# x loaded by halves of its columns, the small first loads on ScalarE's queue, the first weight tile in two halves

## The reference

```python
h = rms_norm(x, a_norm[layer])
att = diff_attention(h, a_w_qkv[layer], ...)     # begins with h @ w_qkv, then norms and rotations of q and k
x = x + att @ a_w_o[layer]
```

## Time and profile before

| | |
|---|---|
| time, median of 3 runs | 1870.19 us (1869.36 to 1870.36) |
| span of the profiled execution, first to last instruction | 1867.2 us |
| median of the timed runs less that span | 3.0 us |
| TensorE busy | 1783.1 us (95%) |
| VectorE busy | 1111.0 us (60%) |
| ScalarE busy | 926.1 us (50%) |
| GpSimd busy | 281.4 us (15%) |
| mean granted TensorE clock | 0.983 |

### The profile page before, as it was taken

How to read it: one execution, slowest core, us unless ns; L and a number is a source line. 1 busy time by engine, 2 the same in 40 slices (tenths; PEclk the granted TensorE clock), 3 DMA queues, 4 the chain that set the end, 5 groups by cost and what they waited for, 6 DMA issues and landing times.

```text
span 1867.2 us, 23188 instructions
## 1 busy us (share of the span) xinstructions
PE 1783.1 (95%) x9282; PEld 1497.2 (80%) x9282; DVE 1111.0 (60%) x1473; ACT 926.1 (50%) x1202; POOL 281.4 (15%) x209
## 2 busy tenths in 40 slices
PE   7778999979999999999999999999999999999997
PEld 5557999868887779998888887888888888888886
DVE  6676655666666656555476474655565667546554
ACT  5354444545655555444564545544455454554442
POOL 2620000066678610000200000000012000000000
PEclk9889999989999999999999999999999999999999
DMA  7223555443433425555754543555665544535561
GB/s 256 91 90 105 192 195 185 159 148 124 135 118 131 136 68 196 188 180 177 241 188 160 177 161 113 177 184 186 196 207 181 174 169 158 180 110 195 188 194 68
DMA packets 158746, 302.64 MB, mean 162 GB/s; under 512 B 5467, under 2 KB 52960, under 8 KB 158640
## 3 DMA queue, kind: packets, MB, share of 16 engines
q1 hardware_dynamic: 157520, 297.16, 47.9%
q0 software_dynamic: 1120, 4.00, 0.8%
HBM read 300.09 MB, written 1.05 MB: 161 GB/s over the span
## 4 chain that ended last, share of the span: by engine, by line
PE 81%; DVE 10%; ACT 4%; POOL 2%; issue 2%; DMA 0%; SPq 0%; DVEq 0%; ACTq 0%; POOLq 0%
PE ps L389 21%; PE ps L391 21%; PE ps L390 21%; PE ps L359 4%; PE ps L581 3%; PE ps L583 3%; PE ps L582 3%; DVE wlo L1217 3%; ACT whi L806 2%; ACT work L886 1%; DVE mx L1298 1%; PE ps L455 1%; PE ps L770 1%; POOL work L1800 1%; DVE st L1283 1%
## 5 line engine op out<-in xcount | busy, mean ns | idle before, releaser
L1217 DVE TENSOR_TENSOR wlo<-raw,whi 128x2048 fp32r<-128x2048 f32 x280 | 657.2, 2352 | 498.5 <-ACT whi L806 498.2
L389 PE MATMUL ps<-whi,hT_hi 128*128 128x512 f32 (+1 forms) x2000 | 794.3, 397 | 8.4 <-DVE wlo L1217 3.8
L391 PE MATMUL ps<-whi,hT_lo 128*128 128x512 f32 (+1 forms) x2000 | 779.4, 390 | 0.0
L390 PE MATMUL ps<-wlo,hT_hi 128*128 128x512 f32 (+1 forms) x2000 | 778.4, 389 | 0.0
L806 ACT ACTIVATE whi<-raw 128x2048 fp32r<-128x2048 f32 x280 | 535.7, 1914 | 387.8 <-PE ps L391 332.0
L389 PEld LDWEIGHTS ps<-whi,hT_hi 128*128 128x128 f32 x2000 | 378.3, 189 | 90.4 <-issue 11.1
L391 PEld LDWEIGHTS ps<-whi,hT_lo 128*128 128x128 f32 x2000 | 377.2, 189 | 79.3
L390 PEld LDWEIGHTS ps<-wlo,hT_hi 128*128 128x128 f32 x2000 | 378.5, 189 | 72.6
L581 PE MATMUL ps<-hT_hi,whi 128*128 128x256 f32 x512 | 145.1, 283 | 0.2
L583 PE MATMUL ps<-hT_hi,wlo 128*128 128x256 f32 x512 | 144.9, 283 | 0.0
L582 PE MATMUL ps<-hT_lo,whi 128*128 128x256 f32 x512 | 144.9, 283 | 0.0
(11 more groups left out here) (162 smaller groups left out, 1224.6 us busy)
## 6 DMA issues: line engine op xcount, KB each, us to landing
raw<-in_w_in SPq DMA_DIRECT2D x46, 1024.0 KB, 5.1
raw<-in_w SPq DMA_DIRECT2D x88, 512.0 KB, 4.5
raw<-in_m_w_up SPq DMA_DIRECT2D x32, 1024.0 KB, 5.2
raw<-in_m_w_down SPq DMA_DIRECT2D x32, 1024.0 KB, 4.9
raw<-in_kv_w SPq DMA_DIRECT2D x24, 1024.0 KB, 5.2
raw<-in_w SPq DMA_DIRECT2D x22, 1024.0 KB, 4.9
raw<-in_a_w_qkv SPq DMA_DIRECT2D x12, 1024.0 KB, 5.8
raw<-in_b_w_q SPq DMA_DIRECT2D x12, 1024.0 KB, 5.1
```

What stands on the lines that cost most here:

```text
L389: pe.matmul(acc, xh, wh, start=start and k == 0, stop=False)
L390: pe.matmul(acc, xh, wl, start=False, stop=False)
L391: ins = pe.matmul(acc, xl, wh, start=False, stop=stop and k == kc - 1)
L1217: vec.tensor_tensor(wlo[:, m % SPLIT, :], raw[:, m % RAW, :], whi[:, m % SPLIT, :], ALU.subtract).then_inc(*mark("lo_ready", ("lo", m)))
```

## The change

The three small first loads move from SyncE to the head of ScalarE's list. x is loaded in four pieces, 512 columns of 128 rows each, and its second half is issued behind tile 0; the turns of a half wait for that half alone. Tile 0 is loaded in two halves (K blocks 0 and 1, then 2 and 3), and ScalarE and VectorE split it in two halves. TensorE begins tile 0 when the first half is split, and waits for the second at K block 2.

```diff
         def x_ready(v, t, n):
-            return ("xload",) if v == 0 else ("x", v, t, n)
+            return ("xload", n) if v == 0 else ("x", v, t, n)
...
         def _(sp):
-            for dst_ap, src, key in ((grows[0:N1, 0, :], a["rows"][0:N1], None), (grows[0:N2, 1, :], a["rows"][N1:N1 + N2], None),
-                                     (ident[:], a_c["c_ident"], ("constants",))):
-                sp.dma_start(dst_ap, src).then_inc(*mark("constants_loaded", key, 16))
-            for t in range(T):
-                last = sp.dma_start(x[:, t, :], a["x"][0, t * P:(t + 1) * P, :])
-                last.then_inc(*mark("x_loaded", ("xload",) if t == T - 1 else None, 16))
             for m, (kc, cols, srcs) in enumerate(tiles):
...
+                if m < 2:
+                    for t in range(T):
+                        last = sp.dma_start(x[:, t, m * 512:(m + 1) * 512], a["x"][0, t * P:(t + 1) * P, m * 512:(m + 1) * 512])
+                        last.then_inc(*mark(f"x_loaded{m}", ("xload", m) if t == T - 1 else None, 16))
+                if m == 0:
+                    src = srcs[0][0]
+                    sp.dma_start(view[:, 0:2], src[:, 0:2]).then_inc(*mark("first_half_landed", ("landed half",), 16))
+                    sp.dma_start(view[:, 2:4], src[:, 2:4]).then_inc(*mark(f"tile_landed{slot}", ("landed", 0), 16))
+                    continue
...
-                pe.wait_ge(*at("lo", m))
+                pe.wait_ge(*(at("lo", m) if m else at("lo half")))
...
+                            if m == 0 and t == 0 and k == 2:
+                                pe.wait_ge(*at("lo", 0))
...
+            def split_first():
+                for half, landed, key in ((slice(0, 1024), ("landed half",), ("hi half",)), (slice(1024, 2048), ("landed", 0), ("hi", 0))):
+                    act.wait_ge(*at(*landed))
+                    sc.activation(whi[:, 0, half], raw[:, 0, half], CP).then_inc(*mark("hi_ready", key))
...
+            for dst_ap, src, key in ((grows[0:N1, 0, :], a["rows"][0:N1], None), (grows[0:N2, 1, :], a["rows"][N1:N1 + N2], None),
+                                     (ident[:], a_c["c_ident"], ("constants",))):
+                act.dma_start(dst_ap, src).then_inc(*mark("constants_loaded", key, 16))
...
             x_half(0, 0)
-            split(0)
+            split_first()
             x_half(0, 1)
...
+            def split_first():
+                for half, landed, hi, lo in ((slice(0, 1024), ("landed half",), ("hi half",), ("lo half",)),
+                                             (slice(1024, 2048), ("landed", 0), ("hi", 0), ("lo", 0))):
+                    dve.wait_ge(*at(*landed))
+                    dve.wait_ge(*at(*hi))
+                    vec.tensor_tensor(wlo[:, 0, half], raw[:, 0, half], whi[:, 0, half], ALU.subtract).then_inc(
+                        *mark("lo_ready", lo))
...
             x_half(0, 0)
-            split(0)
+            split_first()
             x_half(0, 1)
```

## The result

The changed kernel takes 1872.26 us (median of 20 runs, 1871.49 to 1873.93) against 1869.71 us before (20 runs beside it, 1868.78 to 1870.66): ratio 1.0015, 95% interval 1.0008 to 1.0021. It is slower by 2.55 us. The spans of the two profiled executions go the same way: 1870.3 against 1867.2.

A forecast was written before the change was run, and what follows sets the result against it. Mostly TensorE work after a start-up chain through x's load, ScalarE and VectorE. Turns 1.55 earlier plus split 0.5 minus later loads 0.2 gives 1.85 us, so 1870.19 becomes 1868.3 us, range 1865.3 to 1872.2.

The forecast's parts named there:

- ident issued at 1.80, landed 6.26 as before: Small loads on ScalarE's queue: ident keeps SyncE's issue and landing times, so the turns of x start at 7.5.
- The rule against the change: First loads: queues share 16 DMA engines, so spreading saves only issue time; priced at gain 1.5 us, time 1868.7.
- The bound above for ident: Latest case for the first turns: ident issued after ScalarE's table load, 1.28 us later, turns at 8.8.
- X: Start of TensorE's turns of x's first half, 9.05 before; forecast 7.5, bounds 6.3 to 8.8.
- the rival by which nothing moves: First loads land as before, set by the chip's start; only the split's 0.5 us or less is left; chance 0.07.
- ScalarE's table load: Rival at ScalarE's start: table load precedes the small loads, ident issued at 3.1, gain only 0.75 us, 1869.4; chance 0.08.
- x by halves: Load of x: first half lands at 5.6, latest 6.6, so ident sets the turns at 7.5, 1.55 us earlier.
- Both come earlier by between 0 and 1.47: x half 1 and tile 1, landing 11.55 and 14.15 at the same bytes before, were to come that many us earlier.
- Tile 0 in halves: ScalarE and VectorE split of tile 0: saves about 0.5 us on the chain at lo of tile 1.
- From there to lo of tile 2 is VectorE work of fixed length: VectorE between lo of tile 1 and tile 2 (19.83 to 29.30): gain passes through whole, tile 2 at 27.4.
- TensorE's clock: Rival at tiles 2 and 3: 2.2 us wait drops the clock; a 3.4 us fall costs 1.7; chance 0.12 including later stretches.
- The rival that the clock helps: Half-clock stretches between 60 and 660 us end sooner, each 3.4 us giving another 1.7 us, 1866.6; chance 0.18.

The follow-up runs named there:

- e4: Changed kernel, but SyncE waits for ident before its first load, so ScalarE's small loads have the DMA engines to themselves; profiled span 1869.8 us.
- e2: Kernel before, with only the three small loads moved to ScalarE's queue; ratio to before 1.0022.
- e3: Changed kernel, with the first gain-row load taking 128 rows instead of 113; ratio to before 0.9996.
- e5: Changed kernel with small loads back on SyncE and gain rows as 128 rows, halves kept; ratio to before 0.9993.
- e6: Kernel before, with only the gain rows loaded as 128 rows instead of 113; ratio to before 0.9993.
- e3b: Same kernel as e3, run again for its trace alone; profiled span 1864.9 us, restart at 65.58 in e3 and 66.38 here.
- e10: e3 with VectorE's two waits for the landing of tile 0's halves left out; ratio to before 0.9998.
- e1: Changed kernel with the three small loads back at the head of SyncE's queue, halves kept; ratio to before 0.9995.
- e1b: Same kernel as e1, run again for its trace alone; profiled span 1866.5 us, restart at 66.99.
- e7: Kernel before, with only tile 0 loaded and split in halves; profiled span 1867.6 us.
- e12: Kernel before plus 128 gain rows and tile 0 in halves without VectorE's landing waits, TensorE waiting for whole tile 0; 1866.72 us, ratio 0.9986.
- e9: e1 with TensorE waiting for both halves of tile 0 before its first matmul; profiled span 1868.4 us.
- e8: e5 with all four quarters of x issued ahead of tile 0; ratio to before 0.9993.
- e13: Kernel before, with two tiny clears added on VectorE ahead of lo of tile 0; profiled span 1867.9 us.
- e11: Kernel before, with two waits for long-arrived semaphores added on VectorE ahead of lo of tile 0; profiled span 1867.6 us.

## Why the prediction was wrong

**The step that failed: "ScalarE issues the same three from 0.74 ... so I take SyncE's times: ident issued at 1.80, landed 6.26 as before".** The issue time was right (1.86); the landing was 10.80. The load shares the DMA engines with SyncE's bulk, and its last packets drip behind x and tile 0. e4 (no bulk: 5.95), e2 (the queue alone: 12.83) and e3 (128 rows instead of 113: 6.56) show both halves of it: the sharing, and the gain rows that come one behind the other. In SyncE's own queue they had gone ahead of the bulk. With the rows as 128 only the sharing is left: ident was used 1.8 to 2.0 us after its issue from SyncE's queue (e5, e6) and 4.7 to 5.3 from ScalarE's (e3, e3b, e10).

**The rule against the change was named and priced too low.** I put its price at "as late as the first x block of before (6.6)". Two things were missed: that a small load beside a large one loses time at each of its packets (25 ns alone, 95 beside the bulk), and that the packets were not evenly spread, which the trace of before already showed as 75 small packets in line while x was moving. The bound above for ident (X at 8.8, for another mechanism) was not the upper end; X came at 11.98. Nor was 3.2 us from issue to landing the lower one: in e5 and e6 ident was in use 1.8 and 2.0 us after its issue. That also rules out the rival by which nothing moves because the start sets the landings.

**ScalarE's table load** went behind the three issues, so this rival falls, by the timeline above.

**x by halves.** X at 7.5 came about once ident was in time, at 7.27 and 7.65 in e1 and e1b, but partly by luck. The first half was put at 5.6, at the latest at 6.6, and that was too early: in the changed kernel its second load landed at 1.2 + 6.1 = 7.3, which the late ident hid, and in e1 the turns waited for x and not for ident. "At worst each is about 0.4 late" for the second half was wrong as well: in e1 it was used at 11.72 where X + 3.1 = 10.4 wanted it, 1.3 us late, in e5 2.6. "Both come earlier by between 0 and 1.47" failed in the changed kernel: x's last quarter landed at 12.1 (8.6 us after an issue near 3.5), tile 1 at 4.09 + 10.8 = 14.9, both later than the 11.55 and 14.15 at the same number of bytes before. It is the 113-row load again and not the order: e3 differs from the changed kernel in that load alone, and there the two landed at 9.8 and 12.5, 1.7 ahead of before (10.2 and 13.0 in e10). None of this reached the time of the changed kernel, where nothing waited for them: of the signs of being wrong, "x half 1 landing after 11.5" came true without being the cause.

**Tile 0 in halves.** The mechanism and the 0.5 us at lo of tile 1 were right (e7: 10.35 against 10.78; e10 and e12: tile 2 0.4 us nearer). In the changed kernel hi of tile 1 ended 8.00 behind the turns, where X + 8.0 was forecast, and lo of tile 1 10.39 behind them, where X + 10.3 was. "From there to lo of tile 2 is VectorE work of fixed length" was wrong by 0.43 us: two more steps on VectorE uncovered a hole of 0.47 where there had been 0.04. Tile 2 is 20.29 behind the turns against 20.25: the split is worth nothing.

**The sum as it was.** Turns 2.93 late, lo of tile 1 0.39 nearer to them, hole 0.43 more: 2.93 - 0.39 + 0.43 = 2.97 at tile 2, unchanged at the restart (2.98), 3.1 in the span, 2.55 in the timed medians. That the shift survives was forecast, and holds up to the restart; behind it, spans and medians agree with it within what repeats of one kernel differ by.

**TensorE's clock.** The rival fell for the changed kernel: its wait ahead of tile 2 was 2.41 us (forecast 2.2) and the clock stayed. It is real though. Falls of 3.4 us right behind tile 2's start came in e1, e1b, e3b, e5 and e9, after waits of 2.76 to 3.23 us, and in e8 after one of 1.85; none in the changed kernel, e3, e4, e7 and e10, with waits of 1.75 to 2.45. What decides between fall and none at equal waits stays open.

The price was right where it was read and did not last. In e1 tile 3's last matmul ends 41.45 - 28.62 = 12.83 us behind tile 2's start, in e3 39.22 - 27.99 = 11.23: 1.6 us for a fall of 3.4, as against the 1.7 forecast. But the restart is 38.0 us behind tile 2 in all six traces with a fall, and 37.6 in all others where tile 2 was waited for: 0.4 is left. The rest is regained on VectorE, in the twelve small steps between that tile's eviction and the rotation. In order of time, first and last of them in e3, then in e1:

```profile
42.35 0.79 DVE nw L1273
...
48.91 0.19 DVE rqk L1281
```

```profile
44.58 0.55 DVE nw L1273
...
49.94 0.19 DVE rqk L1281
```

They take 6.75 us in e3 and 5.55 in e1. Some of them last 0.5 to 1.2 us instead of 0.19, and all of these begin before GpSimd ends the first rotations (48.42 in e3, 49.03 in e1); behind that each takes 0.19. The rows fit the reading that GpSimd's work stretches these steps, and that steps which come later meet less of it. No run tests that.

The rival that the clock helps came up in the profile and not in the time. The mean granted clock rose from 0.983 to 0.987, and the stretch near 654 us, where it had been 0.51, is gone:

```profile
654.00:661.00 7.00, 4.93 (x39) 3.21 (x38) 1.62 (x5) 3.06 (x8) 2.31 (x2) 1.00 0.41 145
```

Yet the span is longer by the whole shift. The timed runs say the same: of the twenty of the changed kernel, the eight with a granted clock of 0.985 or more average 1872.39 us, the twelve below it 1872.40. So the 1.7 us that I gave to each fall, more or less, is more than these rows show of it in the time.

Behind the restart, spans do not keep its distance: e1b restarts 0.38 us later than e1 and ends 0.2 us earlier, and e3b restarts 0.8 later than e3 and ends 1.0 earlier, so a span by itself says less than a station.

## What to carry to other kernels

Ask of a small load that everything waits for, not when it is issued but what shares its DMA engines: ahead of the bulk in the same queue it was quick, beside the bulk in another queue it took twice as long. Mind its number of rows: 113 came one by one, with 128 that tail was gone, and this one edit moved the restart by 1.1 us in the kernel before and by 3.5 to 4.3 us in the changed one. In those two kernels it also brought the large loads forward, between e1 and e5 it did not. When a split or a reordered load gains time on one engine, count what is next to be late (here x's second half or tile 1, ScalarE, then a hole in VectorE's list) and look at the chain again rather than at the first product, which came earlier in several of these kernels and moved nothing.

## What the runs showed of the hardware that I had not expected

- A load of 64 KB behind a 113-row load: 8.94 us to land beside bulk in another queue (10.89 in e2), 4.17 with no bulk (e4). Its queue's last packets came every 95 to 111 ns instead of every 25.
- As 113 rows instead of 128, the first load delayed ident by 2.6 us (6.26 against 3.64) and x's second row block by 1.1 (0.2 of each by later issue), although it is 56.5 KB. In the changed kernel it delayed x's last quarter and tile 1 by about 2 us (12.1 and 14.9 against 9.8 and 12.5 in e3, 10.2 and 13.0 in e10).
- Small VectorE steps of 0.19 us that lasted up to 1.17 while GpSimd rotated, and 0.19 again from the moment it was done (48.42 us in e3, 49.03 in e1).
- An idle stretch of 0.46 us on VectorE, without a releaser, at a fixed place in its list (ahead of step 61): seen when two tiny steps stand some fifty steps ahead (e13), not seen without them (before) or with one (e11).
